# The norms of a two-layer mixer block: root and reciprocal on four strips of 32 partitions, then spread by small products

## What is computed

```python
def rmsnorm(x, g):
    xf = x.astype(jnp.float32)
    y = xf * lax.rsqrt(jnp.mean(xf * xf, axis=-1, keepdims=True) + EPS)
    return (y * g.astype(jnp.float32)).astype(x.dtype)

def modulate_in(x, g, shift, scale):
    return rmsnorm(x, g) * (1 + scale) + shift
...
    xl = xl + 0.5 * ml[2] * swiglu(modulate_in(xl, g[0], ml[0], ml[1]), f_in[0], f_out[0])
    ol, oc = token_mixer(modulate_in(xl, g[1], ml[3], ml[4]), ...)
    xl = xl + ml[5] * ol
    xl = xl + 0.5 * ml[8] * swiglu(modulate_in(xl, g[2], ml[6], ml[7]), f_in[1], f_out[1])
```

## Time and profile before

| what | value |
|---|---|
| median of 3 runs | 2988.06 us (2987.58 to 2989.79) |
| the profiled execution's own time | 2989.28 us |
| its span in the profile | 2987.6 us |
| PE busy | 2813.4 us, 94% of the span |
| PEld busy | 2539.3 us, 85% |
| DVE busy | 1714.7 us, 57% |
| ACT busy | 853.4 us, 29% |
| POOL busy | 290.7 us, 10% |
| mean granted clock of PE, of full speed | 0.969 |

### The profile page before, as it was taken

One profiled execution on the slowest core, in us unless ns is written; L12 is line 12 of the kernel. 1 busy time (PEld: TensorE's weight loads), 2 busy tenths in 40 slices (PEclk: granted clock), 3 DMA queues, 4 the chain that ended last, 5 costly groups with the idle time before them and its releaser, 6 DMA issues.

```text
span 2987.6 us, 40119 instructions
## 1 busy us (share of the span) xinstructions
PE 2813.4 (94%) x14866; PEld 2539.3 (85%) x14866; DVE 1714.7 (57%) x2888; ACT 853.4 (29%) x1145; POOL 290.7 (10%) x279
## 2 busy tenths in 40 slices
PE   6999999989987799999999899999997987899998
PEld 5999999979844589999999799999986944688887
DVE  7766667669636557766776772222247737633334
ACT  3221122241345442211222422112233256432222
POOL 0000000015322110000000100000004223000000
PEclk8999999999997899999999999999998998999999
DMA  5333233321211013333332232111212311123232
GB/s 205 103 130 131 94 133 125 122 72 56 60 32 46 29 43 124 115 133 107 119 133 107 78 112 72 63 57 63 73 54 86 81 27 41 57 91 104 87 103 80
DMA packets 63377, 264.97 MB, mean 89 GB/s; under 512 B 8881, under 2 KB 11825, under 8 KB 53681
## 3 DMA queue, kind: packets, MB, share of 16 engines
q1 hardware_dynamic: 50608, 180.17, 18.4%
q0 software_dynamic: 11520, 75.11, 7.7%
q10 hardware_dynamic: 1152, 8.39, 0.7%
HBM read 252.89 MB, written 2.10 MB: 85 GB/s over the span
## 4 chain that ended last, share of the span: by engine, by line
PE 83%; DVE 9%; ACT 4%; issue 2%; POOL 1%; DMA 1%; ACTq 0%; SPq 0%; DVEq 0%; POOLq 0%
PE ps L1525 75%; DVE conv_acc L1260 2%; PE ps L1716 1%; PE ps L1782 1%; POOL e_sb L631 1%; DVE w_lo L1008 1%; PE ps L1764 1%; DVE rstd L1061 1%; PE ps L1724 1%; DVE nmax L1366 1%; DMA x<-in_xT 1%; PE ps L1747 1%; DVE y_hi L1097 1%; DVE e_sb L1393 1%; DVE mod_start_acc L1458 1%
## 5 line engine op out<-in xcount | busy, mean ns | idle before, releaser
L1525 PE MATMUL ps<-y_hi,w_hi 128*128 128x384 f32 (+2 forms) x3184 | 906.8, 348 | 71.8 <-DVE w_lo L1008 34.3
L1525 PE MATMUL ps<-y_hi,w_lo 128*128 128x384 f32 (+2 forms) x3184 | 894.8, 344 | 0.0
L1525 PE MATMUL ps<-y_lo,w_hi 128*128 128x384 f32 (+2 forms) x3184 | 894.2, 344 | 0.0
L1525 PEld LDWEIGHTS ps<-y_hi,w_hi 128*128 128x128 f32 x3184 | 583.3, 190 | 114.3 <-issue 44.8
L678 ACT ACTIVATE w_hi<-w_raw 128x1024 fp32r<-128x1024 f32 (+1 forms) x290 | 326.6, 1128 | 1037.1 <-PE ps L1525 1037.1
L1525 PEld LDWEIGHTS ps<-y_lo,w_hi 128*128 128x128 f32 x3184 | 587.1, 190 | 22.3
L1525 PEld LDWEIGHTS ps<-y_hi,w_lo 128*128 128x128 f32 x3184 | 586.8, 190 | 21.0 <-issue 0.5
L1008 DVE TENSOR_TENSOR w_lo<-w_raw,w_hi 128x1024 fp32r<-128x1024 f32 (+1 forms) x290 | 386.2, 1332 | 304.1 <-ACT w_hi L678 300.8
L1023 DVE SCALAR_TENSOR_TENSOR mod_acc<-mod_raw,cact,mod_acc 128x256 f32<-128x256 f32 x896 | 360.1, 477 | 0.0
L1525 PE MATMUL ps<-h_hi,w_hi 128*128 128x384 f32 (+2 forms) x1254 | 354.0, 341 | 0.0
L1525 PE MATMUL ps<-h_hi,w_lo 128*128 128x384 f32 (+2 forms) x1254 | 351.4, 339 | 0.0
(11 more groups left out here) (171 smaller groups left out, 1970.9 us busy)
## 6 DMA issues: line engine op xcount, KB each, us to landing
w_raw<-in_w_up SPq DMA_DIRECT2D x176, 512.0 KB, 3.7
mod_raw<-in_w_mod POOLq DMA_DIRECT2D x64, 1024.0 KB, 5.1
w_raw<-in_w_down SPq DMA_DIRECT2D x64, 704.0 KB, 4.1
w_raw<-in_w_in SPq DMA_DIRECT2D x36, 512.0 KB, 3.6
mod_start<-in_w_mod ACTq DMA_DIRECT2D x8, 1024.0 KB, 22.1
w_raw<-in_w_out SPq DMA_DIRECT2D x16, 512.0 KB, 4.1
stack<-qk_hi SPq DMA_DIRECT2D x48, 96.0 KB, 2.1
band<-in_rpb POOLq DMA_DIRECT2D x16, 224.0 KB, 6.6
```

The lines of the kernel that those rows point to most:

```text
L1525: mm = pe.matmul(slot[s][:, at:at + b - a], w[s][:, k, :], r[:, k, a:b], start=(opens and n == 0), stop=(closes and n == 2))
```

## The change

The sum over the partitions is no longer made on all 128 rows for all tokens. `norm_reduce` makes four matmuls with a stationary matrix of 32 columns, each for a quarter of the half's tokens, into four strips of 32 partitions of PSUM. Root and reciprocal then run on a quarter of the columns (`rquad`). A new function, `norm_spread`, puts the four quarters back on all partitions by four matmuls: the first with one row of ones, the other three with a matrix (`pick`) that has ones in row 32, 64 or 96 alone, made by GpSimd at the start. Its result stays in PSUM (`spread`). DVE multiplies the first half from there; for the second half ACT copies it to `rstd` (`copy_spread`), since GpSimd reads it. The last norm multiplies both halves from PSUM.

The places of the new and moved steps: the spread of the first half stands ahead of unit 1's products on the second half, that of the second half at step 6 of the next phase's first pair; the root of the second half moves from after chunk 4 to after chunk 3 on ACT and also waits for the first spread; its reciprocal from step 6 to step 5 on DVE; the copy stands after chunk 6 on ACT.

```diff
             def root(tokens, half):
                 a, b, _ = halves(tokens)[half]
+                q = (b - a) // 4
                 t.wait("norm_sum")
-                act.activation(rstd[:, a:b], turn[:, LAT * half:LAT * half + b - a], ACT.Sqrt, bias=eps_t[:, 0:1], scale=1.0 / D).then_inc(sems["norm_sqrt"], 1)
+                act.activation(rquad[:, 0:q], roots[half][:, 0:q], ACT.Sqrt, bias=eps_t[:, 0:1], scale=1.0 / D).then_inc(sems["norm_sqrt"], 1)
+
+            def copy_spread(tokens):
+                a, b, _ = halves(tokens)[1]
+                t.wait("spread1")
+                act.activation(rstd[:, a:b], spread[1][:, 0:b - a], ACT.Copy).then_inc(sems["rstd_copied"], 1)
...
             root(TOK, 0)
+            t.wait("spread0")
             root(TOK, 1)
...
-                    if m == 4:
+                    if m == 3:
+                        t.wait("spread0")
                         root(p.tokens, 1)
+                    if m == 6:
+                        copy_spread(p.tokens)
...
                 t.wait("norm_sqrt")
-                dve.reciprocal(rstd[:, a:b], rstd[:, a:b]).then_inc(sems["rstd"], 1)
-                t.wait("rstd")
+                dve.reciprocal(rquad[:, 0:q], rquad[:, 0:q]).then_inc(sems["rstd"], 1)
...
-                        dve.tensor_tensor(sq[m % 2][:, a0:b0], x[:, m, a0:b0], rstd[:, a0:b0], ALU.mult).then_inc(sems["normed0"], 1)
+                        dve.tensor_tensor(sq[m % 2][:, a0:b0], x[:, m, a0:b0], spread[0][:, 0:b0 - a0], ALU.mult).then_inc(sems["normed0"], 1)
...
-                    if m == 6:
+                    if m == 5:
                         invert_root(p.tokens, 1)
...
                 for src, last in ((ssq, False), (sq[1], True)):
                     pe.wait_ge(sems["square" if last else "sum_squares"], (squares_made if last else ssq_made)[0])
-                    mm = pe.matmul(turn[:, LAT * half:LAT * half + b - a], ones[:, :], src[:, a:b], start=not last, stop=last)
+                    for g in range(4):
+                        mm = pe.matmul(roots[half][32 * g:32 * g + 32, 0:q], ones[:, 0:32], src[:, a + q * g:a + q * g + q],
+                                       start=not last, stop=last)
                 mm.then_inc(sems["norm_sum"], 1)
+
+            def norm_spread(tokens, half):
+                a, b, _ = halves(tokens)[half]
+                q = (b - a) // 4
+                t.wait("rstd")
+                for g in range(4):
+                    row, rows = (pick[:, g - 1, :], P) if g else (ones[0:1, :], 1)
+                    mm = pe.matmul(spread[half][:, q * g:q * g + q], row, rquad[0:rows, 0:q], start=True, stop=True)
+                mm.then_inc(sems[f"spread{half}"], 1)
...
+                        if s == 1 and k == 0:
+                            norm_spread(p.tokens, 0)
...
+                                if half == 0 and step == 6 and pair0:
+                                    norm_spread(p.tokens, 1)
...
                     norm_reduce(TOK, 0)
+                    pe.wait_ge(sems["pick"], 4)
+                    norm_spread(TOK, 0)
                     norm_reduce(TOK, 1)
+                    norm_spread(TOK, 1)
```

More of the change, by code:

```diff
@@ L59 @@
 LAG = (4, 5)
+NORMS = 3 * LAYERS + 1
 CONV_A, CONV_G, POOL_U, DIFF_Q, DIFF_K, DIFF_V, NA_Q, NA_K, NA_V = range(0, 18, 2)
@@ L214 @@
     "mod_raw", "mod_sum", "mod_vec", "cond_silu", "mod_step",
-    "hidden_hi", "hidden_lo", "square", "sum_squares", "norm_sum", "norm_sqrt", "rstd",
+    "hidden_hi", "hidden_lo", "square", "sum_squares", "norm_sum", "norm_sqrt", "rstd", "spread0", "spread1", "rstd_copied", "pick",
     "early_done", "updated", "normed0", "normed1", "affine", "y_hi", "y_lo", "scale_ready", "gates_ready",
@@ L296, in trunk @@
     nrsum = place("nrsum", [P, 4])
+    pick = place("pick", [P, 3, P])
     act_buf = place("act_buf", [P, TOK])
@@ L302, in trunk @@
     rstd = place("rstd", [P, POOL_LEN])
+    rquad = rstd[:, 0:LAT // 4]
     at_ssq = cursor[0]
@@ L354, in trunk @@
     outs = ps[:, 3072:4096]
+    roots = [turn[:, 0:LAT // 4], turn[:, LAT // 4:LAT // 2]]
+    spread = [turn[:, LAT:2 * LAT], turn[:, LAT // 2:LAT]]
     mod_ps = outs[:, 0:2 * MOD_COLS // QUAD]
@@ L520, in _ @@
             pool.memset(eps_t[:, 1:2], LN_EPS).then_inc(sems["const_rows"], 1)
+            pool.wait_ge(sems["const_rows"], 3)
+            pool.memset(pick[:, :, :], 0.0).then_inc(sems["pick"], 1)
+            for g in range(1, 4):
+                pool.wait_ge(sems["pick"], g)
+                pool.memset(pick[32 * g:32 * g + 1, g - 1, :], 1.0).then_inc(sems["pick"], 1)
+            pool.wait_ge(sems["pick"], 4)
             def fetch_mod(b, wait=True):
@@ L636, in normalize @@
                 norms[0] += 1
-                pool.wait_ge(sems["rstd"], 2 * norms[0])
+                pool.wait_ge(sems["rstd_copied"], norms[0])
                 for m in range(DC):
@@ L731, in _ @@
                 act.activation(w_hi[s][:, 0:DC, :], raw[s][:, 0:DC, :], ACT.Copy).then_inc(sems["split_hi"], 1)
+            copy_spread(TOK)
             make_y(0, 0, TOK)
@@ L1507, in _ @@
                     invert_root(LAT, 1)
+                dve.wait_ge(sems[f"spread{half}"], NORMS)
                 for m in range(DC):
-                    dve.scalar_tensor_tensor(o_final[:, m, a:b], x[:, m, a:b], gain_f[:, m:m + 1], rstd[:, a:b],
+                    dve.scalar_tensor_tensor(o_final[:, m, a:b], x[:, m, a:b], gain_f[:, m:m + 1], spread[half][:, 0:b - a],
                                              ALU.mult, ALU.mult).then_inc(sems["final"], 1)
@@ L1868, in _ @@
             norm_reduce(LAT, 1)
+            norm_spread(LAT, 1)
 def _feature_major(a):
```

## The result

| | before | after |
|---|---|---|
| median of the runs, us | 2989.38 (6 runs, 2987.58 to 2990.21) | 3002.2 (6 runs, 2999.4 to 3004.66) |
| ratio to before | | 1.0046, 95% interval 1.0036 to 1.0056 |
| span of the profiled execution, us | 2987.6 | 3001.3 |
| DVE busy, us | 1714.7 | 1690.9 |
| PE busy, us | 2813.4 | 2826.3 |

What follows compares the result with a forecast made beforehand. Dense products, untouched by the change, were 75% of the chain that ended last. Start +5.5, norms +1.2, -1.0 and +1.4, end +1.8 gave +8.9 us on 2989.28: 2998.2, the median 1.2 under, 2997.0 us; range 2986.5 to 3008.

Steps and rivals of the forecast that it cites:

- The start: First norm: PE waits twice for reciprocals, so 64 modulation matmuls and the first vector come late; +5.5 us, bounds +0.6, +9.5.
- the clock's two cases: At the program's start: the 64 matmuls take 11.4 us as before, +4.2 us, or 14.0 at low clock, +6.8.
- Sum on strips: PE's sum of each norm half in 16 short passes: 1.2 us, bounds 0.7 and 1.8.
- Spread: PE's eight passes putting the quarters back on all partitions: 1.2 us for 128 columns, 1.0 for 64.
- The norms after down: Second, fourth and fifth norm: early first chunk mostly lost, copy late; 0.4 us slower each, +1.2 for three, bounds -2.3, +6.5.
- The norms after mix_out: Layer 0: first chunk earlier, 1.0 us faster; layer 1: spread waits as long, reciprocal saves less, 1.4 us slower.
- The end: Last norm: first spread adds to PE's path, DVE waits for the last spread at half clock; +1.8 us, bounds +0.6, +2.6.
- The faster rival: Reciprocals' saving gets through if the second spread is done when ACT comes to its copy; -10.6 us, 2977.5 us, chance 8%.

Runs made afterwards that it cites:

- the run with one strip: Changed kernel with eight more matmuls, all on the first strip, ahead of each norm's sum except the last: 3009.97 us.
- the combined kernel: Changed kernel, start's second sum and spreads later, five norms' second reciprocal and spread earlier, last reciprocal among output chunks, end's first spread later: 2980.3 us, again 2983.15.
- the earlier spread: Changed kernel with the second reciprocal one chunk earlier and the second spread at step 4 instead of 6 in the five norms between phases: 2995.45 us.
- the first control: Kernel before the change with only its second-half reciprocal one chunk earlier: 2998.76 us, and 3000.73 us in a second run.
- the first spread earlier: The combined kernel with the first spread of the five norms two steps earlier in the first unit: 2982.2 us.
- the placement late: Changed kernel with the first norm's second sum and both spreads later in PE's queue, and a tile for each half's roots: 2994.78 us.

## Why the prediction was right, and where it was not

The direction and the size came out: +8.9 us forecast, +12.8 measured, inside the range. By its own terms:

- **The start,** +5.5 forecast, +6.4 of its own. The steps happened as told: two waits, the third block at 43.07 (41 to 44 was named), the vector at 63.77 (60 to 64). I took the middle between the clock's two cases, 4.2 and 6.8; the low clock was the right one. (Without the late x the vector would be at 62.8.) The third block takes 13.76 us in the timeline of after, 11.56 before.
- **Sum on strips,** 1.2 forecast with bounds 0.7 and 1.8. Measured 0.57 at 128 columns, below the bound. The step that failed is taking the factor 2.2 of two strips for four, plus entries on both sides. Of the two rules of the Trainium skill (TensorEngine Tiling, Key Properties) that I set against each other, the one that tiles on different columns run in parallel is what the run with one strip shows. Of the drain at a change of the tiling mode no large cost shows: the next full-width product starts 0.33 us after the last eight passes on strips began (625.93, 626.26).
- **Spread,** 1.2 and 1.0 forecast, 1.1 and 1.2 measured at the full clock, 2.2 to 2.3 at half. Root 0.37, reciprocals 0.95 and 0.55, copy 0.38, and the multiplication from PSUM 0.69 as from SBUF: as priced.
- **The norms after down,** +1.2 forecast, 1.23 + 0.62 + 0.02 = +1.9 measured. The total is near by two errors that cancel, and by the draw of the clock (A alone was +0.6 and +0.9 in the other two traces). The sum was 0.6 us too dear and the update came 0.5 us early (8.6 us after `scale`, 9.1 before). But I put the copy 0.4 us late, and it makes ACT's chunk 7 1.3 us late at A: there PE's products ran at the low clock (0.43 us from one 512-column product to the next, not 0.23) from 638 on, which I had at the full clock. At D, at the full clock, nothing is lost.

```profile
638.45 0.63 PE L1551 MATMUL ps<-y_hi,w_lo 128*128 128x512 f32 x1
638.88 0.63 PE L1551 MATMUL ps<-y_lo,w_hi 128*128 128x512 f32 x1
...
2248.69 0.39 PE L1551 MATMUL ps<-y_hi,w_lo 128*128 128x512 f32 x1
2248.92 0.39 PE L1551 MATMUL ps<-y_lo,w_hi 128*128 128x512 f32 x1
```

- **The norms after mix_out,** -1.0 and +1.4 forecast, -0.36 and +1.68 measured, within their bounds. That E is so near its forecast is luck: with the same code it took 29.86 and 29.87 us in two other traces, +0.5, and the rest is the low clock, which I had not priced there. In both ACT waits over 3 us before the copy (at E 2.1 in those two traces), where I had counted only the copy's own 0.5; that B gains 0.4 all the same is the first chunk, 4.5 us after `scale` (1093.31 to 1097.76) and 6.3 before.
- **The end,** +1.8 forecast. The spread costs PE 1.28 us (the last update waits 4.68 instead of 3.40) and the last spread 0.98: +2.3. The other 1.1 us of the stretch from E lie ahead of that spread; up to the update before the last, this stretch is 349.4 us long before and 350.5 after, and 348.9 to 351.0 in the other traces, so I don't put them on the change.

The faster rival said that it decides at the copy. It did: with the spread at step 4 the copy no longer waits, and in that trace the norms are 9.2 us shorter than before the change. What neither I nor the rival had is that this is a matter of two numbers in the order.

## What to carry to other kernels

Cutting a long operation into cheap pieces on another engine pays only if each piece stands in that engine's queue where its input is just ready: ask of every added instruction what it waits for and what stands behind it. Here the same pieces are 0.4% slower or 0.2% faster by their places in the queues (and a tile of its own for each half's roots, which the later places need). And when a change gives time back in untouched code, cut both traces at common events before explaining the total.

## What the runs showed of the hardware

**The same code, 335 or 344 us.** The stretch between norms D and E (the mixer of layer 1 and its projections) is the same in all kernels here, yet took 334.9 to 344.2 us in fourteen traces. The traces part at several places there, most at one, in PE's timeline where the scores' first products follow a wait of 1.66 us; first the kernel before, then the combined kernel's second run:

```profile
2400.11 1.10 PE L1677 MATMUL ps<-z,pool_sb 128*128 128x512 f32 x2 [1.66 <-ACT rstd L860]
2401.14 1.55 PE L1716 MATMUL ps<-z 64*128 64x512 f32 x4
```

```profile
2387.70 1.10 PE L1717 MATMUL ps<-z,pool_sb 128*128 128x512 f32 x2 [1.66 <-ACT rstd L880]
2388.72 2.60 PE L1756 MATMUL ps<-z 64*128 64x512 f32 x4
```

By stretch (length, busy us of PE, PEld, DVE, ACT, POOL, granted clock, DMA share, GB/s), again before and combined:

```profile
2405.00:2420.00 15.00, 9.49 (x36) 4.46 (x34) 10.66 (x9) 9.60 (x15) 6.31 (x4) 0.94 0.15 37
```

```profile
2392.00:2407.00 15.00, 15.00 (x33) 7.44 (x32) 8.42 (x7) 5.92 (x9) 5.05 (x3) 0.53 0.00 0
```

The granted clock is at its lower level, 1.2 GHz, over most of that stretch in the one, and hardly in the other (0.53 against 0.94), after the same wait. Over the whole stretch the mean granted clock was 0.935 or 0.936 in the four traces of 334.9 to 335.6 us, 0.920 to 0.924 in the six of 336.3 to 339.7, and 0.901 to 0.905 in the four of 343.1 to 344.2: the 9 us go with the clock. They are 8.2 us of the earlier spread's trace, which has 12.4 us less in its norms but is only 9.9 shorter, and 9.0 of the 9.1 us that the first control's second trace is longer. The kernel alone doesn't fix it: eleven executions of that with the first spread earlier took 2974.68 to 2986.16 us, the shortest at a mean granted clock of 0.973 and the longest at 0.969. What sets which an execution gets stays open, as no run aimed at it.

**Long sums had raised the clock.** Before the change the 128-row sums at the start end in a stretch at the full level, and the 64 matmuls behind them take 11.4 us. The four other traces with long sums there show the same rise, at 33.0 to 34.6 us, and 10.4 to 11.2 us for the 64. The eight traces with sums on strips alone have no record of the clock before 61 us, and the 64 take 13.6 to 14.0 us, also where PE goes on without a wait (the placement late, above). So it is the shorter sums and not the waits. The run with one strip put PE work back there, again with a rise, at 31.9 us:

```profile
29.19 3.12 PE L1568 MATMUL ps<-ssq,ones_r 128*32 128x128 f32 x15 [1.38 <-DVE ssq L1080]
```

But PE then waits for the first reciprocal, the granted clock is back at 0.50 from 35.3 us, and the 64 matmuls, from 43.78 on, take 13.6 us all the same. A saving on PE can cost the clock of what follows. At the end of that run the last spread took 1.50 us (2997.24 to 2998.74), not 2.17; it had about 1 us more of passes shortly ahead, and the record of the clock's fall comes at 2998.1 us, inside it, where the changed kernel's comes at 2990.0, ahead of it.
